# A decoder step on one core: a new order within the turn, and the layout of the sample's probabilities made by small products on TensorE

## The chip, the cores and the metric

The kernel runs on one core of a Trainium2 chip. The metric is the time of one execution on the device in microseconds (us); runs of one kernel are compared by their median.

The core's engines are named as the profile names them: PE is TensorE's matmul, PEld its weight load, DVE is VectorE, ACT is ScalarE, POOL is GpSimd (here it issues the gathers), SP issues most other DMAs.

## What is computed

One inference step of one hybrid decoder layer, on a prompt of 1024 tokens and on a sample batch of 8 sequences with 4 new tokens each. What matters here is the sample's attention over a paged cache of 8192 past tokens per sequence, which runs beside the prompt's attention.

```python
def diff_attend(q, q_pos, k, v, k_pos, lam):
    s = jnp.einsum('bqhcd,bkhcd->bhcqk', q, k).astype(jnp.float32) * (QK_HEAD ** -0.5)
    mask = k_pos[None, :] <= q_pos[:, None]
    s = jnp.where(mask, s, -jnp.inf)
    p = jax.nn.softmax(s, axis=-1)
    a = p[:, :, 0] - lam * p[:, :, 1]
    return jnp.einsum('bhqk,bkhd->bqhd', a, v.astype(jnp.float32))
...
        k_past = cache_k[l, page_table].reshape(bs, past, N_HEADS, 2, QK_HEAD)
        v_past = cache_v[l, page_table].reshape(bs, past, N_HEADS, V_HEAD)
        k_all = jnp.concatenate([k_past.astype(k.dtype), k], axis=1)
        v_all = jnp.concatenate([v_past.astype(v.dtype), v], axis=1)
        o = diff_attend(q, q_pos_s, k_all, v_all, k_pos_s, lam)
```

All data are float32. There are 4 heads, keys and values are 128 wide, a page has 128 tokens, and a sequence has 64 pages. Keys and values of the cache together are 256 groups of 4 pages, 1.05 MB each, 268 MB in all. Around this stand the adaLN modulation, the input projection, the output projection and the channel mixer, which the change does not touch.

## The kernel before

**Stages.** The program has stages that end with all engines meeting. Stage 3 is the attention, from about 430 to 1251 us of the profiled execution. The change lies wholly in it.

**Slots and turns.** Stage 3 is written out as a list of slots. In slot n the kernel takes key group n (of 128) and, from slot `LAG` on, value group n - `LAG`. Sixteen slots (`STEP`) are one turn, the 64 pages of one sequence; b = n // 16 is the turn and s = n % 16 the place in it. Each engine's program is the slots in this order, so each engine does its pieces strictly one after the other, and semaphores tie the engines together.

**What happens to a key group.** POOL gathers it into one of `RK` buffers of `k_ring`; DVE turns it in place (`turn_keys`, L1491, 32 x 32 blocks); PE multiplies it with the queries (`key_group`, L877); ACT copies the scores to `s_rows` (`take_scores`, L1153). A value group is gathered into one of `RV` buffers of `v_ring` and weighed by the probabilities `p_t` (`value_group`, L896). POOL issues the gather of a group when the buffer's last user on PE is done.

**The softmax of the sample, once a turn.** In the turn after a sequence's scores: DVE finds the maximum of each row (`turn_maxima`, `maximum`), PE and DVE spread it over the rows (`turn_max` L905, `spread_max`, `max_to_rows` L909, `negative_max`), ACT takes the exponentials in five pieces (`sample_exps`, L1159), and PE turns the probabilities, a quarter of a sequence (512 columns, 16 pages) at a time (`turn_p`, L920, r = 0 to 3). The rows of the turned quarter hold (head, page of the group, query) mixed, so the quarter goes to `p_t` by 16 copies of 32 partitions, 8 by ACT and 8 by DVE (`keep_p`, both through `regroup`, L441). Then `fold_sums`, `keep_sums` and `keep_scale` prepare the sums, and `scale_output`, `by_query` and `keep_output` finish the sequence before.

**The dense work.** From slot 6 to slot 141 the prompt's attention is dealt out over the same slots: for each head 2 slots of preparation and 8 units of 4 slots, one unit for each 128 queries, with up to 1024 keys. In the four slots q of a unit stand: q = 0, the first component's scores on PE (`scores`, L833), its maxima on DVE (L1433 to L1435), its exponentials on ACT (`exps`, L1137); q = 1, the same for the second component; q = 2, `combine` on DVE (L1441 to L1446); q = 3, `turn_rows` on PE (L842) and a copy on ACT (L1145). In the next q = 0 PE weighs the values (`weigh_rows`, L853). The result of one engine is what the next waits for, so each unit is a chain through three engines.

**What sets the order in a slot.** On DVE a slot begins with the turning of the next key group, then come the softmax pieces of the turn, then the dense piece. On PE the dense piece comes first, then the key group, the value group, and the softmax pieces. On ACT the order is the copy of q = 3, `take_scores`, the softmax piece, and then the dense exponentials.

Of the kernel before, what the change touches and what calls it, by code (L numbers as in the profile page):

```python
# [36 lines left out]
P = 128  # L37
QUAD = 32
# [74 lines left out]
def build(nc, z, io, const_at, n_const):  # L113
# [6 lines left out]
    GP, RK, RV = 4, 4, 4  # L120
# [3 lines left out]
    LAG = STEP + 7  # L124
    SLOTS = NK + LAG + 2
# [8 lines left out]
    with ExitStack() as ctx:  # L134
# [27 lines left out]
        def sem(name):  # L162
# [191 lines left out]
        p_turned, p_by_act, p_by_dve, sums_folded, folded = (  # L354
            sem("p_turned"), sem("p_by_act"), sem("p_by_dve"), sem("sums_folded"), sem("folded"))
# [79 lines left out]
        def regroup(copy, j, r):  # L435


            got = psum[QUAD * j:QUAD * (j + 1), TURNED, :].rearrange("p (g h a q) -> p g h a q", h=H, a=4, q=8)
            to = p_t[:].rearrange("p (g j) (h q) -> p g j h q", j=4, q=8)
            for a in range(4):  # L440
                last = copy(to[QUAD * a:QUAD * (a + 1), 4 * r:4 * (r + 1), j], got[:, :, :, a, :])  # L441
            return last

# [13 lines left out]
        def load_pages(pool):  # L457
# [217 lines left out]
        def _(pe):  # L675
# [206 lines left out]
            def value_group(m):  # L882
# [7 lines left out]
                if g % 4 == 0:  # L890
                    pe.wait_ge(p_by_act, REVS * e + g // 4 + 1)
                    pe.wait_ge(p_by_dve, REVS * e + g // 4 + 1)
# [44 lines left out]
            def slot(n):  # L937
# [7 lines left out]
                if 1 <= b <= B:  # L945
                    if s == 1:
                        turn_max(b - 1)
                    elif s == 2:
                        max_to_rows(b - 1)
                    elif 4 <= s < 4 + REVS:  # L950
                        turn_p(b - 1, s - 4)
                    if s == 5:
                        fold_sums(b - 1)
                if s == 8 and b >= 2:
# [115 lines left out]
        def _(act):  # L1070
# [90 lines left out]
            def keep_p(e, r):  # L1161
# [11 lines left out]
            def slot(n):  # L1173
                b, s = n // STEP, n % STEP
                if n < NK:
                    take_scores(n)
                if 1 <= b <= B:
                    if s == 2:
                        sample_exps(b - 1)
                    elif 4 <= s < 4 + REVS:  # L1180
                        keep_p(b - 1, s - 4)
                if s == 8 and b >= 2:
                    keep_output(b - 2)

            for n in range(SLOTS):
                h, u, q = dense_at(n)
                if q == 3:
                    keep_turned(u)
                slot(n)
                if u is not None and q == 0:  # L1190
                    exps(u, 0)
                elif u is not None and q == 1:
                    exps(u, 1)
# [84 lines left out]
        def _(dve):  # L1278
# [265 lines left out]
            def slot(n):  # L1544
                b, s = n // STEP, n % STEP
                if n + 1 < NK:
                    turn_keys(n + 1)
                if s == 0 and 1 <= b <= B:
                    maximum(b - 1)
                if s == 0 and b < B:  # L1550
                    new_scores(b)
                if b < B:
                    if s in (4, 8, 12):
                        turn_maxima(b, s // 4 - 1)
                    elif s == 10 and b + 1 < B:
                        queries(b + 1)
                if 1 <= b <= B:
                    if s == 1:
                        spread_max(b - 1)
                    elif s == 2:  # L1560
                        negative_max(b - 1)
                    elif 4 <= s < 4 + REVS:
                        keep_p(b - 1, s - 4)
                    if s == 5:
                        keep_sums(b - 1)
                if s == 6:
                    if b >= 2:
                        scale_output(b - 2)
                    if 1 <= b <= B:
                        keep_scale(b - 1)  # L1570

            queries(0)
            turn_keys(0)
            for n in range(SLOTS):
                h, u, q = dense_at(n)
                if u is None and q == 0:
# [5 lines left out]
                elif q == 0 and u % NT:  # L1582
                    take_rows(u - 1)
                elif n == HEAD0 + H * HEAD_SLOTS:
                    take_rows(H * NT - 1)
                slot(n)
                if u is not None and q == 0:
                    maxima(u, 0)
                elif u is not None and q == 1:
# [210 lines left out]
```

## Time and profile before

| what | value |
|---|---|
| median of 3 runs | 2288.53 us |
| lowest, highest | 2283.9, 2290.83 us |
| the profiled execution's own time | 2287.6 us |
| its span | 2285.7 us |
| stage 3 (first gather to last value group) | 430 to 1250 us |
| busy in the span | PE 1814.9 us (79%), DVE 1088.3 us (48%), ACT 515.8 us (23%) |
| mean granted clock of PE | 0.882 |

How to read it: the span is the profiled execution from its first to its last instruction, and 1.9 us lie around it. Busy shares are means over stages that have different limits, so they say little about stage 3 by themselves. The granted clock is a share of PE's full 2.4 GHz; 0.5 is its lower level, 1.2 GHz.

### The profile page before, as it was taken

How to read it: one execution, taken by the hardware profiler on the slowest of the kernel's cores; microseconds unless marked ns; L12 is line 12 of the kernel's file. 1: busy time of each engine (PE TensorE's matmuls, PEld its weight loads, DVE VectorE, ACT ScalarE, POOL GpSimd, SP SyncE). 2: the span in 40 equal slices, each digit the busy share in tenths (PEclk: the TensorE clock that was granted, in tenths of full speed). 3: DMA queues.
4: the chain of work that ended last, by engine and by line, in shares of the span. 5: the costliest groups of instructions: out<-in, count | busy, mean ns of one | idle time of the engine just before them, and what ended most of it. 6: DMA issues, size and time to landing. Idle time of an engine off the chain costs nothing.

```text
span 2285.7 us, 39884 instructions
## 1 busy us (share of the span) xinstructions
PE 1814.9 (79%) x17492; PEld 1483.2 (65%) x17492; DVE 1088.3 (48%) x1724; ACT 515.8 (23%) x1023; POOL 317.7 (14%) x287
## 2 busy tenths in 40 slices
PE   4799999465766666666665793999999999799992
PEld 1378899344554555545544693777777777799991
DVE  2424121477786776767652567111211111465567
ACT  0301121013223222231231204121112110344441
POOL 0000000122332323323221103400000000000003
PEclk7799999677887788778787797999999999899996
DMA  9711132677998989889876410112112121521112
GB/s 307 273 37 37 37 111 92 226 269 279 415 364 353 364 335 401 324 349 380 329 258 249 157 37 19 56 56 71 58 55 92 55 73 37 221 79 43 43 42 94
DMA packets 133275, 404.29 MB, mean 177 GB/s; under 512 B 12153, under 2 KB 76665, under 8 KB 100338
## 3 DMA queue, kind: packets, MB, share of 16 engines
q0 software_dynamic: 37392, 270.55, 30.4%
q1 hardware_dynamic: 93666, 130.67, 16.9%
q8 instruction: 111, 1.82, 0.3%
q10 hardware_dynamic: 2080, 1.05, 0.2%
q14 instruction: 26, 0.21, 0.0%
HBM read 377.79 MB, written 24.51 MB: 176 GB/s over the span
## 4 chain that ended last, share of the span: by engine, by line
PE 67%; DVE 20%; DMA 8%; issue 2%; ACT 2%; SPq 0%; POOL 0%; DVEq 0%; ACTq 0%; POOLq 0%
PE psum L764 27%; PE psum L1049 11%; PE psum L772 10%; DVE k_ring L1491 5%; DMA k_ring<-cache_k,page_idx 4%; PE psum L877 4%; PE psum L896 3%; DVE p_t L441 3%; DMA ada_w<-w_ada 3%; PE psum L833 3%; PE psum L747 2%; DVE soft L1434 2%; PE psum L842 1%; PE psum L853 1%; DVE x_lo L1332 1%
## 5 line engine op out<-in xcount | busy, mean ns | idle before, releaser
L1491 DVE STREAM_TRANSPOSE k_ring<-k_ring 128x2048 f32<-128x2048 f32 x128 | 294.5, 2303 | 31.1 <-DMA k_ring<-cache_k,page_idx 30.8
L764 PE MATMUL psum<-x_hi,w_hi 128*128 128x512 f32 x896 | 281.6, 396 | 0.0
L764 PE MATMUL psum<-x_lo,w_hi 128*128 128x512 f32 x896 | 277.7, 391 | 0.0
L764 PE MATMUL psum<-x_hi,w_lo 128*128 128x512 f32 x896 | 276.3, 390 | 0.0
L1351 DVE TENSOR_TENSOR w_lo<-w_raw,w_hi 128x2048 fp32r<-128x2048 f32 x37 | 86.9, 2350 | 363.4 <-ACT w_hi L1107 353.8
L1049 PE MATMUL psum<-d_hi,h_hi 128*128 128x256 f32 x704 | 203.2, 289 | 12.7 <-DVE d_lo L1745 12.7
L1049 PE MATMUL psum<-d_lo,h_hi 128*128 128x256 f32 x704 | 200.6, 285 | 0.0
L1049 PE MATMUL psum<-d_hi,h_lo 128*128 128x256 f32 x704 | 200.5, 285 | 0.0
L877 PE MATMUL psum<-k_ring,q_blocks 128*32 128x128 f32 x4096 | 179.8, 331 | 25.3 <-DVE k_ring L1491 24.5
L833 PE MATMUL psum<-k_t,q_zero 128*128 128x512 f32 (+3 forms) x192 | 104.2, 663 | 119.6 <-ACT e_rows L1137 115.6
L764 PEld LDWEIGHTS psum<-x_hi,w_hi 128*128 128x128 f32 x896 | 165.8, 188 | 44.7 <-issue 5.3
L764 PEld LDWEIGHTS psum<-x_hi,w_lo 128*128 128x128 f32 x896 | 168.8, 188 | 35.8
L764 PEld LDWEIGHTS psum<-x_lo,w_hi 128*128 128x128 f32 x896 | 168.9, 188 | 35.6
L877 PEld LDWEIGHTS psum<-k_ring,q_blocks 128*32 128x32 f32 x4096 | 133.9, 132 | 76.5 <-issue 36.3
L461 POOL DMA_INDIRECT k_ring<-cache_k,page_idx x128 | 120.4, 940 | 453.4 <-PE psum L877 436.0
L772 PE MATMUL psum<-w_hi,x_hi 128*128 128x256 f32 x640 | 183.3, 286 | 0.0
L772 PE MATMUL psum<-w_hi,x_lo 128*128 128x256 f32 x640 | 182.2, 285 | 0.0
L772 PE MATMUL psum<-w_lo,x_hi 128*128 128x256 f32 x640 | 182.1, 285 | 0.0
L896 PE MATMUL psum<-v_ring,p_t 128*32 128x128 f32 x4096 | 165.2, 312 | 11.2 <-DMA v_ring<-cache_v,page_idx 8.9
L1744 DVE TENSOR_TENSOR h_lo<-h_all,h_hi 128x1024 fp32r<-128x1024 f32 x88 | 107.6, 1222 | 115.4 <-ACT d_hi L1269 115.4
L896 PEld LDWEIGHTS psum<-v_ring,p_t 128*32 128x32 f32 x4096 | 139.0, 129 | 21.4 <-DMA v_ring<-cache_v,page_idx 9.8
L1049 PEld LDWEIGHTS psum<-d_hi,h_hi 128*128 128x128 f32 x704 | 136.3, 194 | 22.3 <-issue 17.0
(228 smaller groups left out, 2585.3 us busy)
## 6 DMA issues: line engine op xcount, KB each, us to landing
ada_w<-w_ada SPq DMA_DIRECT2D x12, 2048.0 KB, 9.1
w_raw<-w_in SPq DMA_DIRECT2D x12, 1024.0 KB, 5.3
w_raw<-w_gate SPq DMA_DIRECT2D x11, 1024.0 KB, 5.4
w_raw<-w_up SPq DMA_DIRECT2D x11, 1024.0 KB, 6.2
h_store<-h_out SPq DMA_DIRECT2D x11, 1024.0 KB, 7.8
h_all<-h_store SPq DMA_DIRECT2D x11, 1024.0 KB, 8.9
d_raw<-w_down SPq DMA_DIRECT2D x44, 256.0 KB, 2.9
x_rows<-x_prompt SPq DMA_DIRECT2D x2, 2048.0 KB, 16.7
```

What stands on the lines that cost most here:

```text
L441: last = copy(to[QUAD * a:QUAD * (a + 1), 4 * r:4 * (r + 1), j], got[:, :, :, a, :])
L461: pool.indirect_dma_start(to.rearrange("p s d -> p (s d)"), None, rows, bass.IndirectOffsetOnAxis(page_idx[:, n:n + 1], 0)).then_inc(lande ...
L747: last = mm(psum[q:q + QUAD, 4 + s, 0:WB], x_t_s[:, k, :], w_raw[:, s, k, :], start=k < 4, stop=k >= KC - 4)
L764: last = mm(psum[:, 2 * ft + c, 0:CH], w[:, s, k, ft * P:(ft + 1) * P], x[:, k, c * CH:(c + 1) * CH], start=k == 0 and j == 0, stop=k == K ...
L772: last = mm(psum[:, t % TB, 0:WB], x[:, k, t * P:(t + 1) * P], w[:, s, k, :], start=k == 0 and j == 0, stop=k == KC - 1 and j == 2)
L833: last = mm(psum[:, ROWS + k0 // BANK, 0:w], q_zero[:, c, i * P:(i + 1) * P], k_t[:, k0:k0 + w], start=True, stop=True)
L877: last = mm(psum[QUAD * h:QUAD * (h + 1), n % 2, 0:P], q_blocks[:, n // STEP % 2, h, d, :], k_ring[:, n % RK, :, h * HD + d * QUAD:h * HD ...
L896: last = mm(psum[QUAD * h:QUAD * (h + 1), ACC, 0:P], p_t[:, g * GP + j, :], v_ring[:, m % RV, j, h * HD:(h + 1) * HD], start=False, stop=g ...
L1049: last = mm(psum[:, down_bank(par, pair), (t % 2) * WB:(t % 2 + 1) * WB], x[:, s, t * P:(t + 1) * P], w[:, s, :], start=k == 0 and j == 0 ...
L1351: v.tensor_tensor(w_lo[:, s], w_raw[:, s], w_hi[:, s], ALU.subtract).then_inc(w_lo_done, 1)
L1491: v.transpose(group, group).then_inc(k_turned, 1)
L1744: v.tensor_tensor(h_lo[:, s, :], h_all[:, k, :], h_hi[:, s, :], ALU.subtract)
```

## The change

1. DVE's order in a slot: the softmax piece, the dense piece, and last the turning of a key group, now that of slot n + 2 and no longer of n + 1 (three groups are turned before slot 1 instead of two).
2. ACT's order in a slot: `keep_p` and `keep_output`, the dense piece, `take_scores`, and last `sample_exps`.
3. The softmax pieces move later in the turn, so that what one engine makes in slot s another takes in slot s + 1: `turn_max` on PE from s = 1 to 2 and `spread_max` on DVE from 1 to 3, `max_to_rows` from 2 to 3 and `negative_max` from 2 to 4, `sample_exps` from 2 to 4, `turn_p` from 4..7 to 5..8, `keep_p` from 4..7 to 6..9, `keep_sums` from 5 to 7, `scale_output` from 6 to 8, `maximum` from 0 to 1. `LAG` goes from 23 to 24.
4. `turn_p` no longer turns 4 blocks of 128 x 128. It makes 64 products per quarter: 32 columns of `s_rows` as weights, and as the moving operand the 32 columns of the identity that belong to one page of the group. The output lands in `p_t`'s layout.
5. So `keep_p` is one ACT copy of 128 x 512 per quarter, and DVE has no part in it.
6. The rings: `RK` 4 to 5, `RV` 4 to 3 (the sum stays 8 buffers). A value gather is now issued two slots ahead of its slot and no longer three; a key gather four slots ahead of its product, two ahead of its turning.

```diff
-    GP, RK, RV = 4, 4, 4
+    GP, RK, RV = 4, 5, 3
...
-    LAG = STEP + 7
-    SLOTS = NK + LAG + 2
+    LAG = STEP + 8
+    SLOTS = NK + LAG + 3
...
-            for n in range(NK + LAG):
+            for n in range(NK + LAG + RK - RV):
...
-                if n >= LAG:
-                    m = n - LAG
+                if n >= LAG + RK - RV:
+                    m = n - LAG - (RK - RV)
...
                 if REVS * e + r:
-                    pe.wait_ge(p_by_act, REVS * e + r)
-                    pe.wait_ge(p_by_dve, REVS * e + r)
+                    pe.wait_ge(p_kept, REVS * e + r)
                 pe.wait_ge(exp_done, e * (REVS + 1) + r + 1)
                 s_e = s_rows[e % 2]
-                for g in range(4):
-                    at = r * BANK + g * P
-                    last = turn(psum[:, TURNED, g * P:(g + 1) * P], s_e[:, at:at + P], ident)
+                of_page = ident.rearrange("p (h a q) -> p a h q", a=4, q=8)
+                for g in range(0, BANK, QUAD):
+                    for a in range(4):
+                        last = mm(psum[QUAD * a:QUAD * (a + 1), TURNED, g:g + QUAD], s_e[:, r * BANK + g:r * BANK + g + QUAD],
+                                  of_page[:, a], start=True, stop=True)
                 last.then_inc(p_turned, 1)
...
-                for j in range(2):
-                    last = regroup(copy, j, r)
-                last.then_inc(p_by_act, 1)
+                copy(p_t[:, 16 * r:16 * (r + 1), :].rearrange("p g n -> p (g n)"), psum[:, TURNED, :]).then_inc(p_kept, 1)
...
+            for n in range(SLOTS):
+                h, u, q = dense_at(n)
                 b, s = n // STEP, n % STEP
+                if 1 <= b <= B and 6 <= s < 6 + REVS:
+                    keep_p(b - 1, s - 6)
+                if s == 10 and b >= 2:
+                    keep_output(b - 2)
+                if u is not None:
+                    if q == 3:
+                        keep_turned(u)
+                    elif q < 2:
+                        exps(u, q)
                 if n < NK:
                     take_scores(n)
...
+                if 1 <= b <= B and s == 4:
+                    sample_exps(b - 1)
...
-            def keep_p(e, r):
-                dve.wait_ge(p_turned, REVS * e + r + 1)
-                if e:
-                    dve.wait_ge(v_used, STEP * (e - 1) + 4 * (r + 1))
-                for j in range(2, 4):
-                    last = regroup(v.tensor_copy, j, r)
-                last.then_inc(p_by_dve, 1)
...
             queries(0)
             turn_keys(0)
+            turn_keys(1)
             for n in range(SLOTS):
                 h, u, q = dense_at(n)
-                if u is None and q == 0:
+                softmax_piece(n // STEP, n % STEP)
...
+                if n + 2 < NK:
+                    turn_keys(n + 2)
```

Three places show the order. The first is DVE in the turn that holds key groups 32 to 47, around the quarters of the second sequence's softmax; `L441 ... x8` is DVE's half of one quarter's copies, and each `k_ring` row is one key group turned. Before:

```order
L1491 STREAM_TRANSPOSE k_ring<-k_ring 128x2048
L1498 TENSOR_REDUCE dec<-s_rows_97 128x1
L441 COPY p_t<-psum 32x4x32 x8
L1433 TENSOR_TENSOR psum<-psum,consts 128x128
L1434 TENSOR_REDUCE soft<-psum 128x1
L1435 TENSOR_SCALAR soft<-soft 128x1
L1491 STREAM_TRANSPOSE k_ring<-k_ring 128x2048
L441 COPY p_t<-psum 32x4x32 x8
L1528 COPY p_new<-psum 32x32
L1530 TENSOR_REDUCE dec<-psum 128x1
L1433 TENSOR_TENSOR psum<-psum,consts 128x128
```

The same stretch on DVE after the change (the lines have moved by 16):

```order
L1417 TENSOR_TENSOR psum<-psum,consts 128x128
L1418 TENSOR_REDUCE soft<-psum 128x1
L1419 TENSOR_SCALAR soft<-soft 128x1
L1475 STREAM_TRANSPOSE k_ring<-k_ring 128x2048
L1482 TENSOR_REDUCE dec<-s_rows_97 128x1
L1417 TENSOR_TENSOR psum<-psum,consts 128x128
L1418 TENSOR_REDUCE soft<-psum 128x1
L1419 TENSOR_SCALAR soft<-soft 128x1
L1475 STREAM_TRANSPOSE k_ring<-k_ring 128x2048
```

The copies are gone, and the dense maxima stand ahead of the turning of the slot.

The second place is PE in the same turn, around the first two quarters. Before:

```order
L877 MATMUL psum<-k_ring,q_blocks 32x128 x16
L896 MATMUL psum<-v_ring,p_t 32x128 x16
L920 MATMUL psum<-consts,s_rows_97 128x128 x4
L833 MATMUL psum<-k_t,q_zero 128x512
L833 MATMUL psum<-k_t,q_zero 128x128
L877 MATMUL psum<-k_ring,q_blocks 32x128 x16
```

After:

```order
L868 MATMUL psum<-k_ring,q_blocks 32x128 x16
L886 MATMUL psum<-v_ring,p_t 32x128 x16
L910 MATMUL psum<-consts,s_rows_97 32x32 x64
L868 MATMUL psum<-k_ring,q_blocks 32x128 x16
L886 MATMUL psum<-v_ring,p_t 32x128 x16
L910 MATMUL psum<-consts,s_rows_97 32x32 x64
```

Four turnings of 128 x 128 are 64 products of 32 x 32, one slot later in the turn.

The third place is ACT around the first sequence's exponentials in the turn of key groups 32 to 47. Before:

```order
L1159 ACTIVATE s_rows_96,dec<-s_rows_96,dec 128x512 x4
L1159 ACTIVATE s_rows_96,dec<-s_rows_96,dec 128x32
L1137 ACTIVATE e_rows,soft<-psum,soft 128x256
L1153 COPY s_rows_97<-psum 128x128
L1137 ACTIVATE e_rows,soft<-psum,soft 128x256
L1153 COPY s_rows_97<-psum 128x128
L441 COPY p_t<-psum 32x4x32 x8
```

After:

```order
L1128 ACTIVATE e_rows,soft<-psum,soft 128x256
L1144 COPY s_rows_97<-psum 128x128
L1128 ACTIVATE e_rows,soft<-psum,soft 128x256
L1144 COPY s_rows_97<-psum 128x128 x2
L1150 ACTIVATE s_rows_96,dec<-s_rows_96,dec 128x512 x4
L1150 ACTIVATE s_rows_96,dec<-s_rows_96,dec 128x32
L1136 COPY a_t<-psum 128x256
L1144 COPY s_rows_97<-psum 128x128
L1156 COPY p_t<-psum 128x512
```

The five sample exponentials have moved behind both dense exponentials of the unit, and one copy stands where eight did.

## Rows read from the trace of the kernel before

**Rows 1.** The page, share of the 16 DMA engines in 40 slices of 57 us.

```profile
DMA  9711132677998989889876410112112121521112
```

**Rows 2.** Windows of stage 3: length, busy times, granted clock, DMA share, GB/s.

```profile
430.00:1250.00 820.00, 530.70 (x9390) 405.55 (x9390) 563.27 (x962) 195.79 (x631) 240.31 (x256) 0.79 0.87 335
558.00:1162.00 604.00, 403.56 (x7563) 315.66 (x7566) 438.94 (x737) 150.29 (x487) 190.14 (x203) 0.82 0.91 359
775.00:800.00 25.00, 17.04 (x316) 13.64 (x317) 17.68 (x23) 7.21 (x21) 7.60 (x9) 0.81 1.01 418
640.00:645.00 5.00, 5.00 (x83) 4.25 (x82) 1.68 (x2) 0.98 (x3) 1.27 (x2) 0.63 0.18 39
```

**Rows 3.** Waits in 430 to 1250 us: who for whom, total, times, longest.

```profile
PE psum L842 <- DVE a_rows L1446: 124.2, 30, 8.5
PE psum L833 <- ACT e_rows L1137: 115.6, 32, 6.7
...
DVE p_t L441 <- PE psum L920: 75.2, 23, 5.9
...
DVE k_ring L1491 <- DMA k_ring<-cache_k,page_idx: 30.8, 22, 5.1
```

**Rows 4.** Timeline of one turn's quarters: start, duration, engine, line, idle before.

```profile
628.06 2.42 DVE L441 COPY p_t<-psum 32x128 f32<-32x128 f32 x8 [4.84 <-PE psum L920]
...
634.27 2.42 DVE L441 COPY p_t<-psum 32x128 f32<-32x128 f32 x8
...
639.48 1.33 PE L842 MATMUL psum<-consts,a_rows 128*128 128x128 f32 x5 [8.27 <-DVE a_rows L1446]
...
642.98 0.94 POOL L461 DMA_INDIRECT k_ring<-cache_k,page_idx  x1 [11.22 <-PE psum L877]
```

**Rows 5.** Timeline of PE: starts of key groups 0, 20, 24, 32, 36, 40, 100, 104, 112.

```profile
442.98 1.94 PE L877 MATMUL psum<-k_ring,q_blocks 128*32 128x128 f32 x32 [6.69 <-DVE k_ring L1491]
...
525.05 1.08 PE L877 MATMUL psum<-k_ring,q_blocks 128*32 128x128 f32 x32
...
558.12 1.08 PE L877 MATMUL psum<-k_ring,q_blocks 128*32 128x128 f32 x32
...
595.70 1.08 PE L877 MATMUL psum<-k_ring,q_blocks 128*32 128x128 f32 x32
...
614.63 1.08 PE L877 MATMUL psum<-k_ring,q_blocks 128*32 128x128 f32 x32
...
646.86 1.08 PE L877 MATMUL psum<-k_ring,q_blocks 128*32 128x128 f32 x32
...
997.29 0.97 PE L877 MATMUL psum<-k_ring,q_blocks 128*32 128x128 f32 x28
...
1028.77 0.97 PE L877 MATMUL psum<-k_ring,q_blocks 128*32 128x128 f32 x28
...
1064.85 1.08 PE L877 MATMUL psum<-k_ring,q_blocks 128*32 128x128 f32 x32 [0.77 <-DVE k_ring L1491]
```

**Rows 6.** Timeline of PE: key group 127's value group and the next slot's.

```profile
1161.09 1.93 PE L896 MATMUL psum<-v_ring,p_t 128*32 128x128 f32 x64
```

**Rows 7.** Groups of instructions: count, busy us, mean ns, idle before.

```profile
L441 DVE COPY p_t<-psum 32x128 f32<-32x128 f32 x256 | 74.5, 291 | 78.5 <-PE psum L920 75.2
L441 ACT COPY p_t<-psum 32x128 f32<-32x128 f32 x256 | 65.1, 254 | 49.7 <-PE psum L920 47.1
L920 PE MATMUL psum<-consts,s_rows 128*128 128x128 f32 x128 | 22.6, 303 | 2.6 <-ACT p_t L441 2.6
L1145 ACT COPY a_t<-psum 128x512 f32<-128x512 f32 x4 | 2.3, 578 | 11.6 <-PE psum L842 11.6
```

**Rows 8.** Timeline of PE: the new keys' 16 products (32 passes).

```profile
683.43 0.48 PE L866 MATMUL psum<-k_new_t,q_blocks 128*32 128x32 f32 x32
```

**Rows 9.** The tiles `k_ring`, then `v_ring`: their gathers' time to landing.

```profile
DMA to landing us min/median/max: 5.9/9.8/16.3
...
DMA to landing us min/median/max: 5.5/9.6/18.1
```

More of the change, by code:

```diff
@@ L353, in build @@
             sem("max_spread"), sem("max_back"), sem("negmax_ready"), sem("exp_done"))
-        p_turned, p_by_act, p_by_dve, sums_folded, folded = (
-            sem("p_turned"), sem("p_by_act"), sem("p_by_dve"), sem("sums_folded"), sem("folded"))
+        p_turned, p_kept, sums_folded, folded = (
+            sem("p_turned"), sem("p_kept"), sem("sums_folded"), sem("folded"))
         o_scaled_ready, o_t_done, o_t_kept = (
@@ L433, in chain @@
             return link, loop
[L435 to L442, printed above, removed]
         def rope(x1_, x2_, cos, sin, tmp, link, done):
@@ L945, in slot @@
                 if 1 <= b <= B:
-                    if s == 1:
+                    if s == 2:
                         turn_max(b - 1)
-                    elif s == 2:
+                    elif s == 3:
                         max_to_rows(b - 1)
-                    elif 4 <= s < 4 + REVS:
-                        turn_p(b - 1, s - 4)
-                    if s == 5:
+                    elif 5 <= s < 5 + REVS:
+                        turn_p(b - 1, s - 5)
+                    if s == 6:
                         fold_sums(b - 1)
-                if s == 8 and b >= 2:
+                if s == 9 and b >= 2:
                     by_query(b - 2)
@@ L1171, in keep_output @@
                 copy(o_t_all[:, f, :], psum[:, MISC, 448:448 + H * S]).then_inc(o_t_kept, 1)
-            def slot(n):
+            for n in range(SLOTS):
+                h, u, q = dense_at(n)
                 b, s = n // STEP, n % STEP
+                if 1 <= b <= B and 6 <= s < 6 + REVS:
[7 more added lines that the diff above has]
+                        exps(u, q)
                 if n < NK:
                     take_scores(n)
[L1177 to L1193, printed above, removed]
+                if 1 <= b <= B and s == 4:
+                    sample_exps(b - 1)
             stage_end(act, 3)
@@ L1542, in scale_output, with softmax_piece @@
                 dve.wait_ge(o_scaled_ready, f + 1)
[L1544 to L1550, printed above, removed]
-                    new_scores(b)
[L1552 to L1556, printed above, removed]
+            def softmax_piece(b, s):
+                if s == 1 and b < B:
+                    new_scores(b)
                 if 1 <= b <= B:
                     if s == 1:
+                        maximum(b - 1)
+                    elif s == 3:
                         spread_max(b - 1)
-                    elif s == 2:
+                    elif s == 4:
                         negative_max(b - 1)
-                    elif 4 <= s < 4 + REVS:
-                        keep_p(b - 1, s - 4)
-                    if s == 5:
+                    elif s == 7:
                         keep_sums(b - 1)
-                if s == 6:
+                if s == 8:
                     if b >= 2:
@@ L1570, in slot @@
                         keep_scale(b - 1)
+                if b < B:
+                    if s in (5, 9, 13):
+                        turn_maxima(b, s // 4 - 1)
+                    elif s == 11 and b + 1 < B:
+                        queries(b + 1)
             queries(0)
             turn_keys(0)
+            turn_keys(1)
             for n in range(SLOTS):
                 h, u, q = dense_at(n)
-                if u is None and q == 0:
+                softmax_piece(n // STEP, n % STEP)
+                if n == HEAD0 + H * HEAD_SLOTS:
+                    take_rows(H * NT - 1)
+                elif u is None and q == 0:
                     if h:
@@ L1581, in _ @@
                     take_head_queries(h)
[L1582 to L1587, printed above, removed]
+                elif q == 0:
+                    if u % NT:
+                        take_rows(u - 1)
                     maxima(u, 0)
-                elif u is not None and q == 1:
+                elif q == 1:
                     maxima(u, 1)
-                elif u is not None and q == 2:
+                elif q == 2:
                     combine(u)
+                if n + 2 < NK:
+                    turn_keys(n + 2)
             stage_end(dve, 3)
```

3 lines of the change are left out of this document (1 added, 2 removed).

## The prediction

> **What bounds the kernel now.** I read the page first, then the windows, the waits, the timeline and last the gathers' landings. The page's row of DMA shares [rows 1] shows that the transfers matter only in the slices of stage 3, and the diff touches nothing else, so every other stage is taken as it is. The windows [rows 2] give the ceiling of that stage: over 775 to 800 us the DMA engines are full and move 418 GB/s, while over the 604 us in which key and value groups run together (558 to 1162) the mean is 359 GB/s at a share of 0.91. So the transfers are close to the bound, but they stop at times: from 640 to 645 us the share is 0.18. The reader is to see that nothing there is slow; the queue is empty.
>
> Why it is empty, the timeline says [rows 4]. At 628.06 DVE starts its half of a quarter's copies after 4.84 us of waiting for `turn_p`, since both stand in the same slot and PE comes to `turn_p` last in it. Another 2.42 us of copies stand at 634.27. Behind them stands `combine`; PE has its `a_rows` only at 639.48, after 8.27 us of waiting, and POOL's next key gather has by 642.98 waited 11.22 us for PE. The waits say that this is general [rows 3]: PE stands 124.2 us for `combine` and 115.6 us for the dense exponentials in stage 3, whereas DVE stands only 30.8 us for a key gather. The chain PE, DVE, ACT, PE of the dense units bounds the stalled stretches, and the DMA engines bound the rest.
>
> **The pace of the slots** comes from the starts of the key groups [rows 5] and of the last slot [rows 6]. Key group 0 starts at 442.98 and key group 24 at 558.12: 115.1 us for 24 slots. Slot 127 ends half-way through the 1.93 us from 1161.09, at 1162.1: 104 slots in 604.0 us, 5.81 us each. The last value group ends by 1250 [rows 2], 88 us for 23 slots. Within a turn the four slots of the quarters (s = 4 to 7) stand out: from 614.63 to 646.86, 32.2 us for four, and from 997.29 to 1028.77, 31.5 us. Over the five turns between 595.70 and 1064.85 (the first and last are in the rows) these quarters' slots take 151.3 of the 469.15 us, 7.57 us each; the other sixty take 5.30 us each.
>
> **The floor** is two groups of 1.049 MB per slot at 418 GB/s: 5.02 us, 80.3 us a turn. Before, a turn takes 93.8 us.
>
> **The change part by part.**
>
> *The copies.* 256 DVE copies, 74.5 us, and 256 ACT copies, 65.1 us, go [rows 7]. One ACT copy of 128 x 512 per quarter comes; the nearest row is ACT's copy of the same shape from the same memory, 578 ns, so 32 x 0.58 = 18.5 us. ACT has 196 of 820 us busy [rows 2], so this is hidden by its own idle time. If it were not, a slot with a quarter would get 0.58 us longer, against 2.42 us before on DVE, where it wasn't hidden. DVE's wait for `turn_p`, 75.2 us [rows 3], goes with its copies. It is these two, 149.7 us in 32 slots or 4.7 us a slot, that make the quarters' slots long; since they overlap in part with PE's own work, 7.57 - 5.30 = 2.27 us per slot is what shows in the pace.
>
> *The small products.* Before, four turnings cost 22.6 us / 32 = 0.71 us a quarter [rows 7]. After, 64 products in float32 are 128 passes. The nearest row is the new keys' product: 16 products of 32 columns, 32 passes, in 0.48 us at full clock [rows 8], 15 ns a pass, so 1.92 us a quarter, +1.21 us, and +39 us of PE over all. At the lower clock it may be up to twice that. The upper bound is the pace of a key group's passes with 128 columns, 1.08 us for 32 [rows 5], 4.3 us a quarter, +115 us. I take 1.92, since shape and alternation over four column groups are the same. It is hidden by PE's idle time: between 558 and 1162 PE is busy 403.6 of 604 us [rows 2]. Gone that cover, 39 us would come back. The Trainium skill, "TensorEngine Tiling (Array Packing)", section "Instruction Overhead", speaks against such products: it gives each matmul an overhead of about 60 cycles, whatever its columns; an estimate by it would be 25 ns a pass at 2.4 GHz, 3.2 us a quarter, and +80 us of PE where the row gives +39; the row of 15 ns doesn't agree with it, as four column groups may overlap.
>
> *DVE's and ACT's order.* The turning of a key group, 2.3 us, now stands behind the dense maxima and is two slots ahead of its product. So a late turning has a slot of slack before PE needs it, and the dense maxima don't queue behind it. ACT's `sample_exps` moves behind the dense exponentials of its slot; queued behind it are now `keep_turned` or `exps` of the next slot. PE needs `take_scores` of slot n only at slot n + 2. `turn_max` and `spread_max` no longer meet in one slot. I count this as the means by which the quarters' slots fall to the others' pace rather than as an own term, and keep what it may give beyond that for the range: down to the floor, 5.02.
>
> *The rings.* POOL's queue holds key and value gathers in turns; the value gather moves from slot 23's key gather to slot 26's, issued two slots ahead. At 5.3 us a slot that is 10.6 us, against a median of 9.6 us to landing and 18.1 at most [rows 9]. When PE ends a slot, up to three key and three value groups may be on the way, 6.3 MB, 15 us of full transfer, so the engines stay fed while PE slips by a slot. I cost it at nothing; the cover is those buffers, and what it costs if they fall short is the last rival. What is late next is the transfers themselves: DVE should stand for `k_ring` and PE for `v_ring` where before PE stood for `a_rows`.
>
> *`LAG` + 1.* One more slot of values alone at the end and one more of keys alone at the start, fewer with both. It's inside the sums below.
>
> **The sum.**
> - Slots 24 to 127: 104 x (5.30 - 5.81) = -53 us. The floor would give 104 x (5.02 - 5.81) = -82.
> - Slots 0 to 23: the first twenty take 82.1 us (442.98 to 525.05), 4.1 each; the four with quarters take 33.1 (525.05 to 558.12). At 5.3 us, the pace of the other slots once values run too, they take 21.2, and at the first twenty's 4.1 they take 16.4: -12 to -17, taken -14.
> - Values alone: 88 us for 23 slots, 3.8 each. The four with quarters shed 2.27 us each, as above, and there is one slot more: -9 + 4 = -5. Three value buffers and no longer four could take these 5 us back.
>
> Together -72 us. Made against the profiled execution's 2287.6 us that is 2215.6; the median of the runs is 0.9 above that execution, so 2217 us.
>
> **The rivals.**
>
> *The order wins more: the floor.* The dense chain gets so much shorter that the transfers are full throughout: -82 - 17 - 10 = -109, 2180 us (17 and 10 are the far ends of the other two terms). For it speaks that the share is 1.01 for 25 us on end [rows 2]; against it, that the first twenty slots, with keys alone and no quarter, take 4.1 us with the transfers no bound, and a value group adds 1.0 at full clock [rows 6]: at 5.1 us the chain stands level with the floor, and two bounds that alternate make more than either.
>
> *PE takes the place of the copies.* The small products cost near their upper bound, +3.6 us a quarter where I took +1.2, at slots that PE then bounds. 32 x 2.4 = 77 us more of PE; half of it on the path gives back 38: 2255 us. For it: the clock is 0.82 in these 604 us, with stretches at the lower level. Against: PE's third of idle time. By the 60 cycles of the Trainium skill ("TensorEngine Tiling (Array Packing)", section "Instruction Overhead") an estimate would give back at most 41 us, all of it on the path: 2258 us.
>
> *No gain: the stall only moves.* The transfers stand at 0.91 of their time already; if the short stalls regroup at the large units and at the head's preparation, the share stays at 0.91 and so does the pace: 2288 us. Against it: the empty stretches lie in the quarters' slots.
>
> *Slower: the value ring is too short.* A buffer of `v_ring` is used again after three slots. Its cycle is the issue on POOL (1.2 us), the landing, and the wait for and length of the value group (1.5 us): at the median 12.3 us, 4.1 a slot, no bound. It decides from a landing of 3 x 5.81 - 2.7 = 14.7 us on. At the longest landing, 18.1, it is 6.9 us a slot. Were a third of the 104 slots so, it would cost (6.9 - 5.3) x 35 = 56 us and most of the 72 would be eaten; at two thirds it is 2289 - 72 + 112 = 2329 us, the time of this case. Against it: landings that long arise when the queue is full, and then the engines are busy anyway.
>
> **How the numbers follow.** The forecast has 0.58 (2195 to 2240 as its own range), the floor 0.14, PE in the place of the copies 0.15, no gain 0.06, slower 0.07. The range of 8 in 10 runs from 2178, just below the floor, to 2256, PE's case. About 0.3% (7 us) is what a measurement of this kernel can tell from no change: faster 0.88, same 0.05, slower 0.07.
>
> **What would show it.** Right: the key groups' pace between the start of the value groups and slot 127 is 5.1 to 5.4 us, even over the turn; the DMA share there is 0.97 or more; `L910` is about 1.9 us a quarter; ACT's copy 0.58 us; PE's waits for `a_rows` and `e_rows` are far below 240 us, and waits for the rings have grown. Wrong: a share of still 0.91, quarters' slots over 7 us with PE busy in them (the products), or PE standing for `v_ring` with landings over 15 us (the ring). All outside 430 to 1250 us should be the same within 2 us.

## The result

The changed kernel takes 2261.37 us (median of 10 runs, 2254.97 to 2273.98) against 2283.62 us (10 runs, 2278.04 to 2290.83): ratio 0.9903, 95% interval 0.9881 to 0.9924. It is faster by about 22 us, less than a third of the 72 forecast, and outside the range of 2178 to 2256.

The profiled execution of the changed kernel is the fastest of its ten, and the one before lies 4 us over its median. So the two traces differ by 32.5 us of span where the medians differ by 22.

### The profile page after: what moved, and what is told of

The parts are those of the page before. It is cut to its first block, busy times and chain, and to the rows that moved or that the text cites. A ratio compares the mean times of both kernels' runs of the same rounds, so it can differ in the third digit from the quotient of the medians.

```text
span 2253.2 us, 47312 instructions
## 1 busy us (share of the span) xinstructions
PE 1830.4 (81%) x21460; PEld 1499.9 (67%) x21460; DVE 1009.2 (45%) x1468; ACT 466.0 (21%) x799; POOL 321.1 (14%) x287
## 4 chain that ended last, share of the span: by engine, by line
PE 67%; DMA 17%; DVE 8%; issue 5%; ACT 1%; POOL 1%; SPq 0%; DVEq 0%; ACTq 0%; POOLq 0%
PE psum L755 28%; DMA v_ring<-cache_v,page_idx 12%; PE psum L1040 11%; PE psum L763 10%; PE psum L886 3%; DMA ada_w<-w_ada 3%; PE psum L868 3%; PE psum L910 2%; PE psum L824 2%; PE psum L738 2%; DVE k_ring L1475 1%; PE psum L844 1%; DVE x_lo L1316 1%; PE psum L701 1%; DMA k_ring<-cache_k,page_idx 1%
## 5 line engine op out<-in xcount | busy, mean ns | idle before, releaser
L886 PE MATMUL psum<-v_ring,p_t 128*32 128x128 f32 x4096 | 166.6, 307 | 104.8 <-DMA v_ring<-cache_v,page_idx 94.3
L886 PEld LDWEIGHTS psum<-v_ring,p_t 128*32 128x32 f32 x4096 | 130.1, 123 | 127.4 <-DMA v_ring<-cache_v,page_idx 83.9
L868 PE MATMUL psum<-k_ring,q_blocks 128*32 128x128 f32 x4096 | 167.3, 308 | 34.5 <-issue 23.2
L868 PEld LDWEIGHTS psum<-k_ring,q_blocks 128*32 128x32 f32 x4096 | 124.9, 123 | 76.9 <-issue 54.3
L452 POOL DMA_INDIRECT v_ring<-cache_v,page_idx x128 | 121.4, 948 | 193.4 <-PE psum L886 176.7
```

The costliest lines, as they stand in the source:

```text
L452: pool.indirect_dma_start(to.rearrange("p s d -> p (s d)"), None, rows, bass.IndirectOffsetOnAxis(page_idx[:, n:n + 1], 0)).then_inc(lande ...
L868: last = mm(psum[QUAD * h:QUAD * (h + 1), n % 2, 0:P], q_blocks[:, n // STEP % 2, h, d, :], k_ring[:, n % RK, :, h * HD + d * QUAD:h * HD ...
L886: last = mm(psum[QUAD * h:QUAD * (h + 1), ACC, 0:P], p_t[:, g * GP + j, :], v_ring[:, m % RV, j, h * HD:(h + 1) * HD], start=False, stop=g ...
```

## The profile after

The page of the changed kernel: the span and the number of instructions, the share of the DMA engines in 40 slices, and the queue that brings instructions (packets, MB, share of the engines).

```profile
span 2253.2 us, 47312 instructions
...
DMA  9701123487989989898977310121121121621112
...
q8 instruction: 142, 2.33, 0.4%
```

The page before has in the same places:

```profile
span 2285.7 us, 39884 instructions
...
q8 instruction: 111, 1.82, 0.3%
```

There are 7428 instructions more, and 31 packets more in the instruction queue: 0.51 MB, 16 KB each. PE and PEld alone have 7936 records more (21460 each and no longer 17492), which is 31 times 256. The DMA row answers to [rows 1]; it has hardly filled up.

Windows of the changed kernel (length, busy PE, PEld, DVE, ACT, POOL, granted clock, DMA share, GB/s): the stretch with keys and values, then the stages behind.

```profile
558.00:1080.00 522.00, 367.58 (x9257) 288.87 (x9257) 340.07 (x479) 100.67 (x283) 175.22 (x184) 0.87 0.93 372
...
1222.00:2253.20 1031.20, 919.75 (x5774) 788.44 (x5774) 402.44 (x592) 259.91 (x303) 75.97 (x26) 0.94 0.22 73
```

Beside [rows 2], the share went from 0.91 to 0.93 only, and DVE's load fell from 0.73 of the time to 0.65. Behind the last value group the span has 1035.8 us before and 1031.7 now. That is 4 us and not the 2 that were allowed for, but it is scatter: over the traces of all the runs here this part takes 1030 to 1037 us.

Timeline of PE, key groups 0, 24 and 127 of the changed kernel (start, duration, idle before):

```profile
445.08 1.93 PE L868 MATMUL psum<-k_ring,q_blocks 128*32 128x128 f32 x32 [6.91 <-DVE k_ring L1475]
...
544.23 1.08 PE L868 MATMUL psum<-k_ring,q_blocks 128*32 128x128 f32 x32
...
1132.94 1.08 PE L868 MATMUL psum<-k_ring,q_blocks 128*32 128x128 f32 x32
```

Key groups 24 to 127 are 588.7 us apart, 5.72 us a slot. Before, by [rows 5, 6], it was 5.81, and 5.30 was forecast. The first 24 slots take 99.2 us and no longer 115.1: that term was as forecast (-14 forecast, -16 measured).

Waits of the changed kernel in stage 3 (who for whom, total, times, longest):

```profile
ACT p_t L1156 <- PE psum L910: 142.6, 32, 11.0
...
PE psum L886 <- DMA v_ring<-cache_v,page_idx: 94.3, 59, 4.1
...
PE psum L910 <- issue: 53.8, 25, 4.7
...
PE psum L833 <- DVE a_rows L1430: 24.2, 12, 4.6
PE psum L868 <- issue: 23.2, 9, 4.0
DVE k_ring L1475 <- DMA k_ring<-cache_k,page_idx: 20.0, 17, 5.3
...
PE psum L824 <- ACT e_rows L1128: 13.8, 14, 2.2
...
PE psum L886 <- issue: 10.5, 5, 2.8
```

Against [rows 3] the chain of the dense units is gone as a wait: 124.2 and 115.6 us have become 24.2 and 13.8. New are 94.3 us for value groups, and 87.5 us in three rows of `issue`, in which PE waited for nothing that the profile shows. Groups of instructions (count, busy us, mean ns, idle before) show where most of it lies:

```profile
L910 PE MATMUL psum<-consts,s_rows 128*32 128x32 f32 x4096 | 63.1, 211 | 54.8 <-issue 53.8
...
L1156 ACT COPY p_t<-psum 128x512 f32<-128x512 f32 x32 | 18.8, 587 | 142.6 <-PE psum L910 142.6
```

The small products execute in 63.1 / 32 = 1.97 us a quarter, the copy in 0.59: both prices were right (1.92 and 0.58). But PE stands in the middle of a list of products that wait for no semaphore. The timeline of the same turn's quarters as [rows 4]:

```profile
616.47 0.75 PE L868 MATMUL psum<-k_ring,q_blocks 128*32 128x128 f32 x19 [3.01 <-issue]
...
622.38 0.97 PE L910 MATMUL psum<-consts,s_rows 128*32 128x32 f32 x55 [3.54 <-issue]
...
634.95 0.19 PE L910 MATMUL psum<-consts,s_rows 128*32 128x32 f32 x1 [4.67 <-issue]
635.08 2.50 PE L844 MATMUL psum<-v_rows,a_t 128*128 128x128 f32 x10
...
640.26 0.94 POOL L452 DMA_INDIRECT k_ring<-cache_k,page_idx  x1 [10.46 <-PE psum L868]
```

At 634.95 one pass of the 128 is late by 4.67 us, and all that stands behind it on PE; POOL then waits 10.46 us, as it did before the change for another reason.

The packets of the instruction queue say what PE waits for. Each has 16,384 bytes, and the median number of PE's and PEld's records between two of them is 255 from 545 to 1100 us. Their times, from the records of the trace: one starts at 614.0 and ends at 615.1, PE goes on at 616.47; one ends at 621.2, PE goes on at 622.38; one ends at 633.4, PE goes on at 634.95. All 19 gaps of over 1 us inside the lists of small products end 1.2 to 1.6 us after the end of such a packet. Of all 41 idle gaps of PE longer than 2 us in 545 to 1100 us, 23 end 1.0 to 1.7 us after one; before the change 3 of 36 do. And from one of these 23 to the next PE and PEld have a multiple of 256 records, within 2, in 16 of the 22 cases (255, 512, 769, 2049, 2305 and so on): PE stops where one packet's instructions end and the next one's begin.

In the 52 intervals between packets during which the DMA engines were full (a share over 0.97) the least distance is 5.84 us (before: 35 intervals, least 6.1); nearly all nearer ones, down to 3.5 us, stand where the share is lower. So, with full transfers, PE mostly gets no more than 256 instructions in some 6 us. The trace also shows what the 6 us are made of. After the 29 gaps of over 1 us that end with a packet, the next packet starts 3.9 us later at the median where the engines are full until then (18 of them) and 1.5 us later where their share is under 0.9 (9 of them); a packet takes 1.1 us, and PE goes on some 1.4 us after its end. That looks as if each packet were asked for only when PE begins on the 256 instructions before it; the times agree, but no run here tests that.

The Trainium skill, "Advanced Engine Details and Errata", section "ISA Cache", states that instructions are held in lines of 16 KB, 256 instructions; the packets' size and the 256 records between them agree with it. The section speaks of only two lines, and in the same place gives TensorE 128 KB, which would be eight; how many there are no run here shows.

In float32 a product is two passes, and each pass is a weight load and a matmul. A slot's key group and value group are 64 instructions each, the dense work some 15 on the mean, and 64 small products are 256: 400 in a slot with a quarter, 9.4 us of arrival. The four slots of the quarters (`turn_p`, s = 5 to 8) take 9.0 us on the mean of the five turns of key groups 32 to 111; the other twelve take 4.7. That is below the transfers' 5.02, presumably because the rings fill while PE stands.

## The experiments

Two theories. **F**: the order is good, and the small products take it back since PE's instructions arrive too slowly. **R**: three value buffers are too few (PE's 94.3 us for `v_ring`). A third, **X**, is that the products cost what they execute. All ratios are to the kernel before, with 95% intervals; in such terms the changed kernel is 0.9903.

**e1: the order alone.** New order, `LAG` and rings; turnings and copies as before, the copies one slot after the turning.

```diff
-                for g in range(0, BANK, QUAD):
-                    for a in range(4):
-                        last = mm(... of_page[:, a], start=True, stop=True)
+                for g in range(4):
+                    last = turn(psum[:, TURNED, g * P:(g + 1) * P], s_e[:, at:at + P], ident)
...
-                copy(p_t[...], psum[:, TURNED, :]).then_inc(p_kept, 1)
+                for j in range(2):
+                    last = regroup(copy, j, r)
```

> The new order, rings and LAG as in the changed kernel; the quarter is turned by four 128 x 128 turnings and copied by 8 + 8 copies as before (both copies one slot after the turning). Theory F (PE's program arrives too slowly: the profile's instruction queue brings 16 KB at a time, 256 of PE's instructions apart, and no two arrive nearer than about 6.1 us while the DMA engines are full; 64 small products are 256 instructions a quarter): without the products PE's 'issue' gaps fall from about 90 us to under 10, and it is faster than the changed kernel by 15 us or more, 2245 us or less. Theory R (three value buffers are too few): the waits for v_ring stay near 94 us and the time stays at 2255 to 2268.

Measured: 2193.09 us, ratio 0.9599 (0.9582 to 0.9616). A window and a wait of its profile:

```profile
558.00:1080.00 522.00, 375.81 (x7434) 285.80 (x7433) 430.16 (x724) 144.21 (x480) 187.26 (x199) 0.89 1.01 408
```

```profile
PE psum L896 <- DMA v_ring<-cache_v,page_idx: 104.2, 67, 4.1
...
PE psum L920 <- issue: 6.4, 4, 3.8
```

The order brings 4.0%, 92 us. The DMA engines are full over the whole window. PE still waits 104.2 us for `v_ring`, so that wait is a sign of full transfers. `issue` is down to 6.4 us. Both halves of F's expectation hold. R's fails: the wait for `v_ring` is there, the loss is not.

**e2: the products alone,** in the old order, rings and `LAG`, with ACT's one copy.

```diff
-                for g in range(4):
-                    at = r * BANK + g * P
-                    last = turn(psum[:, TURNED, g * P:(g + 1) * P], s_e[:, at:at + P], ident)
+                for g in range(0, BANK, QUAD):
+                    for a in range(4):
+                        last = mm(... of_page[:, a], start=True, stop=True)
```

> The old order, rings and LAG; only the 64 small products a quarter and ACT's one copy are new. Theory F: a slot with a quarter needs some 400 instructions of PE, 9.5 us of arrival, against 7.57 us before: no gain in spite of the copies' 2.4 us and DVE's wait, 2275 to 2320 us. Rival X (the products cost what they execute, 1.9 us): the copies' removal shows, 2235 to 2260.

Measured: 2288.44 us, ratio 1.002 (1.0002 to 1.0038). Taking 74.5 us of copies and their wait from DVE gained nothing; the products took it all. The time lies in F's range and above X's.

**e3: four and four buffers.** `GP, RK, RV = 4, 4, 4` in the changed kernel.

> The changed kernel with four key and four value buffers. Theory R: 15 us or more faster than the changed kernel, 2245 or less, PE's waits for v_ring under 50 us. Theory F: within 7 us of the changed kernel, 2254 to 2268, the 'issue' gaps unchanged near 90 us.

Measured: 2257.21 us, ratio 0.9878 (0.9859 to 0.9897); the interval meets that of the changed kernel. Its waits:

```profile
DVE k_ring L1475 <- DMA k_ring<-cache_k,page_idx: 90.7, 67, 5.2
...
PE psum L886 <- DMA v_ring<-cache_v,page_idx: 8.1, 8, 2.1
```

PE's wait for `v_ring` is 8.1 us and no longer 94.3, DVE's for `k_ring` 90.7 and no longer 20.0; `issue` stays, at 94 us in three rows. The wait moved and the time stayed: R falls.

**e4: the products in sixteenths.** 16 products a slot in every slot, and a copy of 128 x 128 each.

```diff
-                    elif 5 <= s < 5 + REVS:
-                        turn_p(b - 1, s - 5)
...
+                if STEP + 5 <= n < STEP + 5 + NK:
+                    turn_p(n - STEP - 5)
```

> The changed kernel, but the 64 products of a quarter are dealt out over four slots: 16 products a slot in every slot, with an ACT copy of 128 x 128 each (the same number of products in all). Theory F: 206 instructions a slot on the mean, 4.9 us of arrival, under the transfers' 5.02, no burst: 'issue' gaps under 30 us in all, 2205 to 2235 us. Rival X and R: the same work and the same rings, 2250 to 2268.

Measured: 2195.9 us, ratio 0.9623 (0.96 to 0.9646).

```profile
558.00:1080.00 522.00, 385.89 (x10438) 316.25 (x10437) 366.00 (x521) 119.75 (x385) 185.82 (x195) 0.92 1.00 402
```

```profile
PE psum L910 <- issue: 62.5, 31, 3.8
PE psum L885 <- issue: 31.3, 21, 3.2
PE psum L868 <- issue: 30.5, 17, 3.1
```

The same number of small products costs 64 us less when no slot has more than a sixteenth of them. Two expectations failed. The time is below F's 2205 to 2235, within 5 us of e1. And the gaps did not fall: they add up to 124 us against 87, the longest 3.8 us against 4.7. But PE's wait for the transfers, 104.2 us in e1, is down to 20.1 here:

```profile
PE psum L885 <- DMA v_ring<-cache_v,page_idx: 20.1, 17, 3.1
```

So most of the gaps stand where PE would have waited for the transfers anyway. Their sum is no measure of the loss; the burst is.

**e5: 16 of the 64 products** in each quarter (three quarters of them are left out, so the sample's probabilities are incomplete).

```diff
-                for g in range(0, BANK, QUAD):
+                for g in range(0, P, QUAD):
```

> The changed kernel with 16 of each quarter's 64 products (it leaves out three quarters of them, so the sample's probabilities are incomplete). Theory F (arrival of PE's instructions): a quarter's slot has 206 instructions, 4.9 us of arrival, under the transfers' pace, so the whole cost goes: level with the order alone, 2190 to 2203 us. Rival X (a product costs a fixed time): a quarter of the 68 us stays, 2207 to 2215.

Measured: 2183.58 us, ratio 0.9564 (0.9542 to 0.9587), below both ranges. 48 products and 192 instructions fewer a quarter give back 3.4%, 77 us or 2.4 us a quarter, more than the 1.4 us that they execute (63.1 - 17.7 us over 32). The 16 products left cost nothing that shows against e1, which has DVE's copies in their place.

**e6: every product twice.**

```diff
-                for g in range(0, BANK, QUAD):
+                for g in [*range(0, BANK, QUAD), *range(0, BANK, QUAD)]:
```

> The changed kernel with every small product made twice (the output is the same). Theory F: 256 more instructions a quarter, 6.1 us of arrival x 32 = +195 us, 2400 to 2470 us. Rival X: +1.9 us of execution x 32 = +61, or once more the measured 68, 2320 to 2335.

Measured: 2403.58 us, ratio 1.0527 (1.0498 to 1.0555): +6.2%, 142 us, 4.45 us for 256 instructions that execute in 1.6 (114.7 us in all, against 63.1). It lies at the lower end of F's range of times and short of F's +195, and far above X. The DMA share goes with the miss:

```profile
570.00:1200.00 630.00, 426.51 (x12244) 339.55 (x12239) 347.65 (x493) 102.80 (x291) 176.18 (x187) 0.82 0.80 316
```

At a share of 0.80 the engines are idle part of the time, and then packets come as near as 3.3 us to each other. The nearer ones stand in intervals with a share from 0.01 to 0.97, but one at 0.98 (3.6 us), so about 6 us is what full engines mostly give, and no fixed limit.

**e7: more work, few instructions.** Two products of 128 x 512 ahead of each quarter's small ones.

```diff
+                for _ in range(2):
+                    mm(psum[:, TURNED, :], ident, s_e[:, r * BANK:(r + 1) * BANK], start=True, stop=True)
```

> The changed kernel with two products of 128 x 512 ahead of each quarter's small ones, into the same bank (overwritten afterwards, the output is the same): some 1.7 us more of PE's work, as much as the 64 small products execute, but 8 instructions and no 256. Theory F: hidden in the arrival, within 12 us of the changed kernel, 2250 to 2273 us. Rival X: 32 x 1.7 = +54 us, 2300 to 2320.

Measured: 2278.82 us, ratio 0.9992 (0.9971 to 1.0013): +0.9%, 20 us, in neither range: execution alone would give 54, and F gave 12 at most. In the trace the long products take 75.3 us, and the small ones behind them 45.3 and no longer 63.1, so PE's work grows by 57.5 us. Most of it disappears in the arrival, a third does not: when PE is late with a long product, it may also ask later for the next packet. That last reason is argued, not shown.

**e10: instructions without work.** e1, and ahead of each quarter's four turnings 64 products of a single column.

```diff
+                for g in range(0, BANK, QUAD):
+                    for a in range(4):
+                        mm(psum[QUAD * a:QUAD * (a + 1), TURNED, g:g + 1], s_e[:, r * BANK + g:r * BANK + g + QUAD],
+                           ident[:, 0:1], start=True, stop=True)
```

> The new order with the old turnings and copies, and ahead of each quarter's turnings 64 products with 32 columns of weights and one single column moved, into the same bank (overwritten, the output is the same): 256 instructions and next to no columns. Theory F (arrival of instructions): the loss of the changed kernel comes back, 2245 to 2275 us, with PE 'issue' gaps of 60 us or more. Rival: the loss was in the products' columns, in the layout or in ACT's copy: 2193 to 2210.

Measured: 2274.56 us, ratio 0.9957 (0.9942 to 0.9971): 82 us slower than e1, all of the changed kernel's loss (69) and a little more. The expectation of F holds, with 66 us of `issue` in four rows.

```profile
L920 PE MATMUL psum<-consts,s_rows 128*32 128x1 f32 x4096 | 61.5, 180 | 53.6 <-issue 48.9 <-ACT p_t L441 2.0
```

Neither the columns, nor the layout, nor ACT's copy is the cause: these products move one column, write to no layout, and the copies are the old ones. By itself this run doesn't tell arrival from execution, since these 4096 passes execute in 61.5 us too; e4 to e7 do. Of the 13 us over the changed kernel's loss a part may be the clock's: from 558 to 1080 us PE was granted 0.83 here, 0.87 in the changed kernel and 0.89 in e1. No run separates that.

**e8 and e12: no value gathers.** The changed kernel (e8) and e1 (e12), both with three value gathers in all; the loading of the other 125 value groups is left out, and old data are weighed. One run each.

```diff
-                        gather(v_pages, v_ring[:, m % RV], v_in[m % RV], m)
+                    if m < RV:
+                        gather(v_pages, v_ring[:, m % RV], v_in[m % RV], m)
```

> The changed kernel with three value gathers in all (it leaves out the loading of the other 125 value groups and weighs old data): the transfers need 2.5 us a slot. Theory F with the full DMA engines as its cause: instruction packets come as near as 3.4 us to each other, PE's 'issue' gaps fall from 89 us to under 30. Theory F with a fixed rate of arrival: the least distance stays at 6.1 us, the gaps stay at 89 us or grow, since PE waits for nothing else.

> The new order with the old turnings and copies and three value gathers in all (it leaves out the loading of the other 125 value groups). Against 2126.5 us with the small products and no value gathers: if the products cost by the arrival of instructions and that is slow because the DMA engines are full, they cost less here than the 68 us with all gathers, and this takes 2085 to 2115; if the rate of arrival is fixed, they cost 68 or more, since no transfer hides them: 2058 or less.

Measured: 2126.5 us and 2104.94 us. With the DMA engines at shares of 0.62 to 0.67 the products cost 22 us and no longer 69, and in e8 instruction packets come as near as 3.3 us. e12 lies in the range expected for slow arrival under full engines. For e8 half of what was expected failed: the `issue` gaps are still 70 us in four rows, the longest 4.8. So lighter transfers let instructions arrive faster, and yet not at PE's pace.

**e9: the order with four and four buffers.** `GP, RK, RV = 4, 4, 4` in e1.

> The new order with the old turnings and copies (2193 us), but four key and four value buffers. If the transfers are the bound there (share 1.01, 408 GB/s), the rings make no difference: 2186 to 2200 us, with the waits moved from v_ring to k_ring. If the fifth key buffer does the work, over 2205.

Measured: 2186.88 us, ratio 0.9577 (0.9551 to 0.9602), the fastest complete kernel here, though its interval meets e1's. The fifth key buffer isn't needed. Here PE has 31.2 us of `issue` before its turnings (`L920`), the longest 5.5 us, at no cost that shows. All twelve gaps stand ahead of a list and none in one, and they end 3 to 11 us after a packet, so they are not the arrival; what PE waited for there stays open.

**e11: the shift alone.** e1 with the old order within the slot on DVE and ACT, turnings one slot ahead, four and four buffers.

```diff
+                if n + 1 < NK:
+                    turn_keys(n + 1)
                 softmax_piece(n // STEP, n % STEP)
...
-                if n + 2 < NK:
-                    turn_keys(n + 2)
```

> The old order within the slot on DVE and ACT, turnings one slot ahead, four and four buffers, old turnings and copies; only the softmax pieces are shifted so that no two engines meet in one slot, and LAG is 24. If the shift is what empties the quarters' slots, most of the order's 91 us is here: 2193 to 2225 us. If the order within the slot does it: 2250 to 2280.

Measured: 2210.46 us, ratio 0.9684 (0.9663 to 0.9705). Of the order's 4.0 to 4.2%, 3.2% (72 us) are the shift: DVE's wait for `turn_p`, 75.2 us before, is 2.7 us here, since no engine has to wait any more for a piece that another has only in the same slot. The order within the slot brings the last 1.1% (24 us, against e9).

## Why the prediction was wrong

**The step that failed** is the small products: "It is hidden by PE's idle time". The execution was priced right (1.92 us against 1.97), and the bounds, from 1.9 to 4.3 us a quarter, were all bounds of execution. What the products cost is their arrival: 256 instructions, which with full DMA engines mostly take 6 us or more to come, in slots that last 5. The price is 69 us (0.9903 against 0.9599), shown by e1. That it is one of instructions and not of columns, layout or copy shows in e10; that it is not their execution shows in e4 (the same passes, 64 us less), e5 (77 us for 45 of execution), e6 (142 us for 52) and e7 (20 us for 57). PE's idle time is no cover for it, since a PE that waits for instructions is itself idle. [Rows 4 and 8] could not tell: a single list of 16 products is 64 instructions, a quarter of one packet. The page before did have a row that bears on it, the 111 packets of the instruction queue, and I didn't read it.

In the terms of the sum, the products' cost was put at nothing beside the 53 us of slots 24 to 127; in the traces they gave 13 (604.0 to 590.6).

**Bound of the kernel before: right.** e1 fills the transfers: a share of 1.01, 408 GB/s, where [rows 2] had 0.91 and 359.

**The order: right in mechanism, sized too small.** Slots 24 to 127 were to fall from 5.81 to 5.30 us, the other twelve slots' pace; in e1 they fall to 5.12 (key groups 24 and 127 at 543.64 and 1071.24 us), near the floor of 5.02, which had been given a chance of 0.14. The order alone is worth 92 us, not 72. The term was sized by the mean pace of the other twelve slots, 5.30 us, as if it were free of stalls. It wasn't: over the same five turns the slots s = 0, 2 and 8 took 8.1, 7.8 and 8.7 us before, as long as the quarters' slots (8.2, 4.8, 11.8 and 5.4), and in e1 s = 0 and 2 take 5.2 and 5.7. The old order made these stalls too, and so the reason given against the floor, two bounds that alternate, did not hold. With fewer stalls PE's granted clock rose as well (0.82 before, 0.89 in e1); what it added no run separates.

**The copies: right in size, wrong in worth.** They go as said (DVE's 74.5 us, ACT's copy 0.59 us). But in the new order they cost little: e1 keeps them, and e5, without them and with a quarter of the products, is 8 us faster (0.9564 against 0.9599, intervals that just meet), while DVE's wait for the turning falls from 75.2 to 15.8 us. It was the wait in the same slot that was dear, and the shift took it away.

**The rings: right.** The wait for `v_ring` appeared as said and costs next to nothing: with four and four buffers both kernels are faster by 0.2% (e3, e9), with intervals that meet. The gathers' median time to landing rose from 9.6 to 12.0 us for values, which took the slack of the two slots without a cost that shows. The rival of the short ring counted 1.2 us for the issue on POOL; the row has 0.94 ([rows 4]). **Head and end:** -16 us for the first 24 slots against -14; the values alone take from about 1134.8 to 1221.5, 86.7 us against 88, -1 against -5. Key group 0 starts 2 us later than before.

**PE in the place of the copies** was the rival nearest to what happened: 2255 forecast for it, with a chance of 0.15. Its mechanism, the products' execution near the upper bound, was wrong all the same. The 60 cycles of the Trainium skill ("TensorEngine Tiling (Array Packing)", section "Instruction Overhead") do not show in the passes here, which take 15 ns each, and 11 in e7 behind the long products; their estimate of 2258 us came near the measured time without its cause.

## What to carry to other kernels

Count instructions, not only their time. A list of many short instructions on one engine has a price of its own where the transfers are full, here 2.2 to 2.6 us for 256 beyond a slot's share, and idle time of the engine doesn't cover it; the sign is `issue` in the middle of a list that waits for no semaphore, just behind the end of a packet of the instruction queue. An `issue` row by itself is no sign of it (e9), and its sum is no measure of the loss (e4). Dealing the same instructions out evenly over the slots (e4) makes them nearly free: within 5 us of the kernel without them (e1), though e1 has the old copies and e4 has not. In a program of slots, let no engine take a piece in the same slot in which another makes it: this shift alone gave 3.2%.

## What was not expected of the hardware

Instruction packets of 16 KB mostly start 6 us apart or more while the 16 DMA engines are full (least 6.1 us before, 5.8 in the changed kernel, 5.4 in e4; single ones are nearer, 4.2 in e2, 3.6 in e6, 4.1 in e10), and down to 3.3 us when they are partly idle. PE goes on 1.0 to 1.7 us after a packet's end, and the records from one such stop to the next are mostly a multiple of 256. Products of one column take PE as long as products of 32: 61.5 and 63.1 us for 4096 passes. Behind two long products (e7) the same 4096 passes take 45.3 us.
